# A two-layer fp32 streaming encoder on one core: where feed-forward's norm rows, the down projection's first half and one weight piece stand

## What is computed

```python
def rms_norm(x, g):
    y = x32 * lax.rsqrt(jnp.mean(x32 * x32, axis=-1, keepdims=True) + RMS_EPS)
    return (y * g.astype(F32)).astype(x.dtype)

def swiglu(h, w_gate, w_up, w_down):
    return (jax.nn.silu(h @ w_gate) * (h @ w_up)) @ w_down

mem_n = rms_norm(mem, mem_norm_g)
# per layer
kv = (mem_n @ w_kv).reshape(bsz, n_mem, 2, XA_HEADS, XA_HEAD_DIM)
x = x + memory_cross_attention(rms_norm(x, xa_norm_g[layer]), mem_n, ...)
x = x + swiglu(rms_norm(x, f_norm_g[layer]), f_w_gate[layer], f_w_up[layer], f_w_down[layer])
```

## Time and profile before

| | us |
|---|---|
| three runs | 1708.27, 1707.21, 1708.54 |
| median | 1708.27 |
| the profiled execution | 1708.71 |
| its span, first to last instruction | 1706.9 |
| TensorE busy in it | 1648.6 (97%) |
| VectorE busy | 768.2 (45%) |
| ScalarE busy | 623.9 (37%) |
| GpSimd busy | 253.4 (15%) |

### The profile page before, as it was taken

The page is one execution under the profiler, slowest core; times in us unless marked ns, Lnnn a source line. Parts: engine busy times, 40 slices in busy tenths (PEclk is TensorE's granted clock), DMA queues, the critical chain, the costliest instruction groups (busy, mean ns, idle before and its releaser), DMA issues.

```text
span 1706.9 us, 22635 instructions
## 1 busy us (share of the span) xinstructions
PE 1648.6 (97%) x9358; PEld 1343.3 (79%) x9358; DVE 768.2 (45%) x1006; ACT 623.9 (37%) x1010; POOL 253.4 (15%) x315
## 2 busy tenths in 40 slices
PE   5989989999999999999999999999999999999999
PEld 4778788788878788888888887567887788888887
DVE  4658435555444444443225435773453444444222
ACT  6533433344434322221114336564452522222110
POOL 3863034010000211110000003110000011111000
PEclk9999899999999999999999999999999999999999
DMA  6610212034212333332223332322212243333221
GB/s 203 135 50 1 75 52 71 31 123 149 74 49 75 99 98 98 96 97 88 92 95 99 99 123 99 96 78 99 80 45 74 60 113 98 93 93 94 91 98 74
DMA packets 146801, 151.85 MB, mean 89 GB/s; under 512 B 8864, under 2 KB 109344, under 8 KB 146592
## 3 DMA queue, kind: packets, MB, share of 16 engines
q1 hardware_dynamic: 146720, 150.69, 28.9%
HBM read 147.53 MB, written 3.15 MB: 88 GB/s over the span
## 4 chain that ended last, share of the span: by engine, by line
PE 88%; DVE 6%; ACT 4%; issue 2%; POOL 0%; DMA 0%; SPq 0%; DVEq 0%; ACTq 0%; POOLq 0%
PE ps L329 24%; PE ps L331 24%; PE ps L330 24%; PE ps L2070 1%; PE ps L1730 1%; PE ps L425 1%; PE ps L2100 1%; DVE sb L610 1%; PE ps L1707 1%; PE ps L964 1%; DVE w_lo_ab L301 1%; PE ps L2088 1%; ACT sb L1741 1%; ACT sb L2159 1%; PE ps L1242 1%
## 5 line engine op out<-in xcount | busy, mean ns | idle before, releaser
L329 PE MATMUL ps<-h_hi,w_hi 128*128 128x512 f32 x864 | 338.7, 392 | 4.4 <-DVE w_lo L1904 3.9
L330 PE MATMUL ps<-h_lo,w_hi 128*128 128x512 f32 x864 | 337.2, 390 | 0.0
L301 DVE TENSOR_TENSOR w_lo<-raw,w_hi 128x2048 fp32r<-128x2048 f32 x66 | 155.0, 2349 | 341.7 <-ACT w_hi L297 341.7
L297 ACT ACTIVATE w_hi<-raw 128x2048 fp32r<-128x2048 f32 x84 | 160.8, 1915 | 377.1 <-PE ps L331 376.4
L331 PE MATMUL ps<-h_hi,w_lo 128*128 128x512 f32 x704 | 274.4, 390 | 0.0
L329 PEld LDWEIGHTS ps<-h_hi,w_hi 128*128 128x128 f32 x864 | 162.9, 189 | 39.2 <-issue 4.7
L330 PEld LDWEIGHTS ps<-h_lo,w_hi 128*128 128x128 f32 x864 | 162.9, 189 | 33.5
L1904 DVE TENSOR_TENSOR w_lo<-raw,w_hi 128x2048 fp32r<-128x2048 f32 x44 | 138.1, 3139 | 53.5 <-ACT w_hi L1886 53.5
L331 PEld LDWEIGHTS ps<-h_hi,w_lo 128*128 128x128 f32 x704 | 132.5, 188 | 27.8
L1886 ACT ACTIVATE w_hi<-raw 128x2048 fp32r<-128x2048 f32 x44 | 84.3, 1916 | 161.2 <-PE ps L331 161.2
L1914 POOL CAST a_hi<-up 128x512 f32 x44 | 27.0, 613 | 777.2 <-DVE up L1902 777.2
(11 more groups left out here) (378 smaller groups left out, 2697.3 us busy)
## 6 DMA issues: line engine op xcount, KB each, us to landing
raw<-in_f_w_gate SPq DMA_DIRECT2D x44, 512.0 KB, 4.0
raw<-in_f_w_up SPq DMA_DIRECT2D x44, 512.0 KB, 5.2
raw<-in_f_w_down SPq DMA_DIRECT2D x44, 512.0 KB, 4.2
raw<-in_xa_w_kv SPq DMA_DIRECT2D x16, 1024.0 KB, 5.0
raw<-in_c_w_qkv SPq DMA_DIRECT2D x12, 1024.0 KB, 5.1
raw<-in_ab_w_in SPq DMA_DIRECT2D x10, 1024.0 KB, 6.0
raw<-in_xa_w_q SPq DMA_DIRECT2D x8, 1024.0 KB, 5.0
raw<-in_xa_w_out SPq DMA_DIRECT2D x8, 1024.0 KB, 5.0
```

The costliest lines, as they stand in the source:

```text
L297: a.activation(w_hi[:, n % 2, :], raw[n % 2], ACT.Copy).then_inc(sem("w_hi"), 1)
L301: v.tensor_tensor(w_lo(n)[:, n % 2, :], raw[n % 2], w_hi[:, n % 2, :].bitcast(F32), ALU.subtract).then_inc(sem("w_lo"), 1)
L329: pe.matmul(out, a[0], b[0], start=start, stop=False)
L330: pe.matmul(out, a[0], b[1], start=False, stop=False)
```

## The change

Three edits, in code that is written in another order; no instruction is added or removed on any engine.

- `ffn_up_pe`, both layers: the wait for `rinv` and the four matmuls L1864 stand behind the gate half of panel 0 (s == gu == 0), no longer behind its up half.
- `ffn_down_pe`, both layers: for row block 0, column half 1 (banks 4 to 7) is computed before column half 0 (banks 0 to 3). Ahead of the first stands the wait for one product of the up loop less, and the wait for the last product stands between the halves.
- ScalarE's list, layer 0: the copy of `kv00_1` stands between the squares of x's half 0 and those of half 1 (with their tiny Sqrt), no longer behind both.

```diff
@@ -1858,11 +1858,11 @@
             for s in range(2):
                 for gu in range(2):
                     done(group(s, gu, range(4, KT)), gu)
-                if s == 0:
-                    pe.wait_ge(sem(f"f{l}_rinv"), after(f"f{l}_rinv", 1))
-                    for i in range(TT):
-                        ins = pe.matmul(ps[:, 4, i * P:(i + 1) * P], rinv[:, i:i + 1].broadcast_to([P, P]), ident, start=True, stop=True)
-                    ins.then_inc(sem(f"f{l}_rmm"), 1)
+                    if s == gu == 0:
+                        pe.wait_ge(sem(f"f{l}_rinv"), after(f"f{l}_rinv", 1))
+                        for i in range(TT):
+                            ins = pe.matmul(ps[:, 4, i * P:(i + 1) * P], rinv[:, i:i + 1].broadcast_to([P, P]), ident, start=True, stop=True)
+                        ins.then_inc(sem(f"f{l}_rmm"), 1)
 
             with pe.Fori(1, FT // 2) as j:
                 for s in range(2):
@@ -1917,7 +1917,7 @@
 
         def ffn_down_pe(pe, l):
 
-            pe.wait_ge(sem(f"f{l}_free"), after(f"f{l}_free", 2 + FT))
+            pe.wait_ge(sem(f"f{l}_free"), after(f"f{l}_free", 1 + FT))
             for j in range(FT // 2):
                 w = take_split(pe, f"dn{l}_{j}", 2)
 
@@ -1928,7 +1928,9 @@
                 if j < FT // 2 - 1:
                     for k in (2 * j, 2 * j + 1):
                         pe.wait_ge(sem(f"f{l}_alo"), after(f"f{l}_alo", 2 + k + 1))
-                        for half in range(2):
+                        for half in (1, 0) if k == 0 else (0, 1):
+                            if k == half == 0:
+                                pe.wait_ge(sem(f"f{l}_free"), after(f"f{l}_free", 2 + FT))
                             for i in range(TT):
                                 ins = part(k, half, i)
                     ins.then_inc(panel_used, 1)
@@ -2499,7 +2501,9 @@
             norm_root_act(a, "m", MT)
             norm_out_act(a, "m", MT, mem_T, "mem_g", ("abo1_1",))
             pieces_hi(a, "kv00_0")
-            squares_act(a, "x0", x, m_junk, ss2, "mo_x")
+            squares_act(a, "x0", x, m_junk, ss2, "mo_x", (0,))
+            pieces_hi(a, "kv00_1")
+            squares_act(a, "x0", x, m_junk, ss2, "mo_x", (1,))
             for l in range(DEPTH):
                 if l == 1:
                     kv1_norms_act(a)
@@ -2512,7 +2516,6 @@
                     turned_hi_act(a, "x1", "xa_g1", 1)
                     pieces_hi(a, "cao1_1", 2)
                 else:
-                    pieces_hi(a, "kv00_1")
                     norm_root_act(a, "x0", TT)
                     kv_act(a)
                     turned_hi_act(a, "x0", "xa_g0", 1)
```

## The result

The changed kernel takes 1698.62 us, the median of 5 executions (1697.31 to 1699.43). The kernel before takes 1707.21 us in 5 executions (1706.02 to 1708.54). The ratio is 0.9948 with a 95% interval of 0.9934 to 0.9963: 8.9 us are gone (6.3 to 11.3), and the difference of the two medians is 8.6. The forecast was 1699.2, with a gain of 9.1. The profiled execution took 1698.94 us with a span of 1697.1, against 1708.71 and 1706.9 before; the forecast had 1699.6 and 1697.8.

The account below looks back on a forecast made before the run. TensorE, busy 97% of the span, bounds the kernel; only its idle or low-clock time can be won. 1.65 + 4.29 + 2.20 + 1.18 = 9.32, less 0.2, takes 1708.27 to 1699.2 us; range 1697.3 to 1703.0.

Parts of the forecast that it names:

- Part 1: Feed-forward loop entry: rinv's transposes (norm rows) one group earlier save 1.65 us in layer 0, 4.29 in layer 1, less 0.2.
- the tie: Feed-forward loop entry: first subtraction ends just as TensorE needs it, 0.03 us to spare; 0.1 us taken off per layer.
- Part 2: Down projection's start: column half 1 first, last product's wait 12 matmuls later, saves 1.10 us per layer, 2.20 together.
- Part 3: Second key/value piece, layer 0: its copy between the halves of x's squares removes TensorE's wait, saving 1.18 us.
- B: Loop entry: subtraction comes late, 0.3 to 0.8 us stay per layer, perhaps the low clock too; up to 1702.2; chance 0.15.
- C: Loop entry and exit: waits hid equally long instruction fetches, only the key/value gain is left; 1707.1 us; chance 0.06.
- D: Layer 1's attention: the clock falls in more short idle stretches, 1.8 us each; slower, 1711.8 us; chance 0.03.
- E: Layer 1's attention: its one fall of the clock vanishes as well; 1697.4 us; chance 0.07.

Follow-up runs that it names:

- e5: Changed kernel with the four transposes of rinv behind the up half's first 6 matmuls, not the gate half: 0.21 us slower in feed-forward 0, 1.34 in feed-forward 1.
- e8: Kernel before, with GpSimd's a_lo waiting for VectorE's subtraction w_lo of the same half: feed-forward 1 2.69 us shorter, feed-forward 0 unchanged.
- e11: Kernel before with the transposes of rinv later, behind 6 matmuls of the second panel's gate half: 3.00 us slower in feed-forward 0, 1.38 in feed-forward 1.
- e1: Kernel before with only the transposes of rinv moved one group earlier: 1.59 us off feed-forward 0, 4.27 off feed-forward 1, 5.86 in all.
- e12: Changed kernel, with GpSimd's a_lo waiting for VectorE's subtraction w_lo of the same half: median 1697.86 us, ratio 0.9949 to the kernel before.
- e2: Kernel before with only the down projection's new order of halves and later wait: 1.15 and 1.27 us off the two feed-forward stages, 2.42 in all.
- e6: Changed kernel with the full wait back ahead of the down projection, column half 1 still first: 1.15 and 1.18 us slower in the two feed-forward stages.
- e7: Changed kernel with the kv00_1 copy ahead of both halves of x's squares: the key/value stage takes 39.72 us, 1.40 more than with the change.
- e4: The changed kernel itself, run again beside its three parts: 7.5 us gained by ratio (5.1 to 9.7), 9.34 us by the stages.
- e9: The kernel before, unchanged, profiled once more: loop entry waits of 1.38 us in layer 0 and 2.50 to 2.51 in layer 1.
- e10: The kernel before, unchanged, profiled yet again: loop entry waits of 1.38 us in layer 0 and 2.50 to 2.51 in layer 1.
- e3: Kernel before with only the kv00_1 copy moved between the halves of x's squares: 1.21 us off the key/value stage.

## Why the prediction was right, point by point

**Part 1, the first subtraction.** Forecast: copy 0.43 us behind the up half's last matmul, the subtraction 1.95 us behind the copy, 3.12 us long, TensorE just on time. Measured in layer 0: 0.43, 1.95 (554.65, 556.60), 3.13, and TensorE at the common pace. Every start there is 1.65 us before the one forecast, because the forecast was written on the time scale of the kernel before and part 3 (1.20), the start (0.39) and 0.06 in cross0 stand ahead; the distances are the same. The choice that the forecast called the one that matters, 3.12 us and not 2.29 or 3.42, held in both layers, and e5 shows that 3.43 was to be had with the norm rows 6 matmuls later.

**Part 1, the clock.** Forecast: 1.63 us in layer 1, straight behind the idle time. Three experiments make the link between wait and fall, and not only a coincidence in time: e8 shortens the wait from 2.50 to 1.37 us and the fall goes; e11 lengthens layer 0's from 1.38 to 2.73 and a fall comes; e1 takes the wait away and the fall with it. The price is 1.6 us each time. Forecast for part 1 5.94 less 0.2; e1 measured 5.86, 0.12 more. What stays for the tie is about the 0.1 us in each layer that was taken off: 0.08 us by the first matmul of 0.46 to 0.47 us, and e12, which gives the tie more room, gets 0.11 and 0.08 back. Of the 0.12, some hundredths are in the price of the waits, which was a little low (see part 2), and the rest is within the 0.08 us to which a stage repeats. The tie itself was forecast for the matmul alone; the weight load in front of it did come late, which the forecast doesn't speak of and which the 0.1 happened to cover.

**Part 2.** Forecast 2.20 for both layers; 2.42 in e2, and 2.33 from the change to e6. The idle time was priced right (0.83 + 0.16 + 0.11), but a restart costs some hundredths more than its second matmul shows, so that each wait was 1.15 to 1.18 us in e6 and not 1.10: in the kernel before, TensorE's starts are 1.13 us (layer 0) and 1.17 us (layer 1) late from the tenth matmul behind the wait on. That the wait for the last product does no harm 12 matmuls later is seen at once: the product ends at 778.54, and the first matmul that waits for it stands at about 777.60 + 12 x 0.227 = 780.3.

**Part 3.** Forecast 1.18; measured 1.20 to 1.21. The copy came 0.49 us behind the matmul that frees its slot (0.43 forecast), the subtraction ended 0.94 us before TensorE asked, the squares behind it ended at 366.27, and the next copy started at 367.11 with the first piece's last matmul (366.62) as its releaser, not the squares. e7 shows how near the other side was: with all the squares behind the copy, the same gain is lost at the next piece.

**The rivals.** B, the lost tie, didn't occur; e5's layer 1 is what it looks like, 1.34 us, and there without a fall of the clock. C, a fetch of instructions hidden under the waits, is refuted at all places where a wait went: entry 559.66 to 559.89 and 1355.52 to 1355.74, exit 777.37 to 777.60 and 1573.20 to 1573.43, the common pace of 0.23 us. By the rule of the Trainium skill that the prediction cites ("Runtime: NRT & Kernel Launch", section "Instruction fetch mechanics") a fetch could have stood there; the trace of the change shows none. D, more falls in layer 1's attention, didn't occur in 14 profiles. E, that the one fall there vanishes, occurred in 3 of 14: layer 1 takes 442.1 to 442.3 us in eleven of them and 440.6 to 440.7 in e5, e7 and e12. Here is the same stretch of the attention in the change and then in e12, with the wait ahead of it:

```profile
1087.38 0.85 PE L2090 MATMUL ps<-sb 128*128 128x128 f32 x3 [1.87 <-ACT sb L2118]
...
1087.00:1090.00 3.00, 2.62 (x8) 2.23 (x9) 1.45 (x5) 2.93 (x10) 1.23 (x2) 0.58 0.00 0
```

```profile
1088.10 0.55 PE L2091 MATMUL ps<-sb 128*128 128x128 f32 x3 [1.87 <-ACT sb L2119]
...
1087.00:1090.00 3.00, 1.90 (x11) 1.59 (x12) 1.01 (x4) 3.00 (x11) 1.76 (x1) 1.00 0.00 0
```

The wait is the same, 1.87 us; the clock falls in one and not in the other. e4 is the same program as the change and e9 and e10 are the kernel before, and all of these fell; e5, e7 and e12 differ from the change at other places only. Whether their edits play a part through when they arrive there, or it is chance, stays open: each was profiled once. The fall is worth 1.5 us of layer 1 (442.2 against 440.7), where the forecast had 1.8.

**The sum.** Forecast 9.32 less 0.2; the stages give 9.31. The median is 0.6 us below the forecast. The forecast started from 1708.27, the median of three executions of the kernel before; from 1707.21, the median of all five, the same sum gives 1698.1, 0.5 below what was measured. Both differences are within what executions of one kernel spread. In the profiled ones the largest part of that spread is the start, from 359.05 to 362.27 us in code that no version changes. What moves it wasn't studied. The timed gain (8.9 us, and 7.5 in e4) lies a little under the stages' 9.3, with intervals that hold it.

## What to carry to other kernels

Price a wait on the engine that sets the end as its idle time, plus what of the last record would have overlapped, plus the restart, plus the stretch at the lower clock behind it: here the last was 1.6 of the 4.3 us of the dearest one. Work out the new start of everything that is queued behind a moved step, since a step about 1 us later decided whether the gain stayed (e5, e7); a wait can often be put later by first doing the part of the work that doesn't need it (part 2). And measure a small gain by the stage and not by the whole time: 2.4 us of e2 were lost in a spread of 5 us, and plain in its two stages.

## What the runs showed of the hardware

- **Who begins first decides, not both slow down.** A 128x2048 subtraction on VectorE and a 128x512 one on GpSimd that start within 0.02 us of each other take 2.29 and 3.43 us, or 3.43 and 1.29: the later one pays all. If GpSimd is 0.17 us ahead, VectorE takes 3.27 (566.05 against 565.88 in the kernel before), if 0.3 us, 3.12; with a_lo behind the subtraction (e8, e12) they take 2.29 and 1.29. So the later one loses what the other has left to run at that moment, less some 0.15 us. Unexpected was how little decides it, and that it comes out differently in two layers of one program, yet alike in all seven profiles where the two coincide at the entry (before, e2, e3, e5, e9, e10, e11): VectorE is ahead in layer 0, GpSimd in layer 1. Why the order differs there isn't shown.
- **TensorE's clock after idle times at the loop's entry.** After 2.50 us or more it fell in 7 of 7 cases (before, e2, e3, e9 and e10 in layer 1, e11 in both layers), to about 0.5, the lower of the two levels (1.2 GHz), and cost some 1.6 us; after 1.15 to 1.38 us in 0 of 8 (layer 0 of before, e2, e3, e8, e9 and e10, layer 1 of e5 and e8). The attention's wait of 1.87 us among other short ones was followed by a fall in 11 of 14 profiles.
- **A loop's edges.** Entering and leaving TensorE's loop cost nothing that can be seen: the matmuls stay 0.23 us apart across both.
